# The first block's projections, index scores and choice of keys as one list of tiles, with products by sevens and head roots by logarithms

## The reference

```python
    h = rms_norm(x, norm_w) * (1.0 + scale[:, None, :]) + shift[:, None, :]
    p = h @ w_in
    ...
    q, k, v, gb, iq, ik, iw = jnp.split(pb, DSA_SPLITS, axis=-1)
    q = rms_norm(heads(q), q_gain)
    k = rms_norm(heads(k), k_gain)
    yb = dsa_sparse_attention(q, k, v, iq, ik, iw).reshape(B, S, D_ATT)
    yb = (yb * jax.nn.silu(gb)) @ w_b_out
    gm_a, gm_b = jnp.split(pg, 2, axis=-1)
    merged = jax.nn.sigmoid(gm_a) * ya + jax.nn.sigmoid(gm_b) * yb
```

## Time and profile before

| | us |
|---|---|
| median of three runs | 3241.15 |
| the profiled execution | 3241.27 |
| its span, first to last instruction | 3239.4 |
| TensorE busy in the span | 3051.8 (94%) |
| VectorE busy | 1595.6 (49%) |
| ScalarE busy | 721.5 (22%) |
| mean granted clock of TensorE | 0.988 of full |

### The profile page before, as it was taken

The page is one execution under the profiler, slowest core; times in us unless marked ns, Lnnn a source line. Parts: engine busy times, 40 slices in busy tenths (PEclk is TensorE's granted clock), DMA queues, the critical chain, the costliest instruction groups (busy, mean ns, idle before and its releaser), DMA issues.

```text
span 3239.4 us, 41104 instructions
## 1 busy us (share of the span) xinstructions
PE 3051.8 (94%) x17188; PEld 1833.3 (57%) x17188; DVE 1595.6 (49%) x2499; ACT 721.5 (22%) x1220; POOL 9.6 (0%) x10
## 2 busy tenths in 40 slices
PE   7999999999998899998998998999999999999998
PEld 3476544577446633322332323587577887887875
DVE  4553249655957612222221121546586767576664
ACT  3110232413037110100000000100441333241413
POOL 0000000000000000000000000100000000000000
PEclk9999999999999899999999999999999999999999
DMA  8301144131203499999999999322112212221210
GB/s 282 130 3 54 53 162 176 58 117 64 78 23 118 172 428 428 427 428 428 428 428 428 427 428 416 141 78 98 57 53 78 78 53 78 74 83 53 79 52 27
DMA packets 122072, 588.20 MB, mean 182 GB/s; under 512 B 6944, under 2 KB 9248, under 8 KB 97696
## 3 DMA queue, kind: packets, MB, share of 16 engines
q1 hardware_dynamic: 121888, 585.57, 45.3%
HBM read 583.45 MB, written 2.10 MB: 181 GB/s over the span
## 4 chain that ended last, share of the span: by engine, by line
PE 74%; DMA 16%; DVE 7%; ACT 2%; issue 1%; SPq 0%; DVEq 0%; ACTq 0%
PE ps L579 25%; PE ps L594 20%; DMA work<-in_w_up 7%; PE ps L2724 6%; DMA weight_ring<-in_w_up 5%; PE ps L2805 4%; DMA spare_slot<-in_w_up 3%; PE ps L598 2%; PE ps L2687 2%; PE ps L1389 2%; PE ps L3414 1%; PE ps L1914 1%; PE ps L1903 1%; PE ps L3434 1%; PE ps L3399 1%
## 5 line engine op out<-in xcount | busy, mean ns | idle before, releaser
L594 PE MATMUL ps<-hT,weight_ring 128*128 128x512 f32 (+1 forms) x1016 | 448.9, 598 | 2.9 <-ACT work L707 1.2
L594 PEld LDWEIGHTS ps<-hT,weight_ring 128*128 128x128 f32 (+1 forms) x1016 | 191.5, 191 | 238.2 <-issue 233.3
L365 DVE TENSOR_TENSOR work<-work,ps 128x512 f32<-128x512 f32 x203 | 139.4, 687 | 228.6 <-PE ps L579 224.3
L579 PE MATMUL ps<-weight_ring 128*128 128x256 f32 x992 | 224.8, 379 | 0.0
L2724 PE MATMUL ps<-work 128*64 128x512 f32 x832 | 189.3, 597 | 23.9 <-DMA work<-in_w_up 16.6
L594 PE MATMUL ps<-work,weight_ring 128*128 128x512 f32 (+1 forms) x496 | 211.1, 572 | 0.0
L2889 DVE SCALAR_TENSOR_TENSOR xT<-ps,mod,xT 128x512 f32<-128x512 f32 x128 | 96.1, 751 | 232.3 <-PE ps L2738 222.5
L2724 PE MATMUL ps<-weight_ring,work 128*64 128x512 f32 x800 | 183.4, 602 | 22.4 <-DMA weight_ring<-in_w_up 13.3
L579 PEld LDWEIGHTS ps<-weight_ring 128*128 128x128 f32 x992 | 186.9, 190 | 24.8
L579 PE MATMUL ps<-weight_ring,spare_slot 128*128 128x256 f32 x800 | 181.6, 380 | 0.0
L579 PE MATMUL ps<-hT,weight_ring 128*128 128x256 f32 x736 | 167.2, 383 | 6.3 <-DVE hT L800 3.8
(11 more groups left out here) (491 smaller groups left out, 4266.8 us busy)
## 6 DMA issues: line engine op xcount, KB each, us to landing
work<-in_w_up SPq DMA_DIRECT2D x27, 2048.0 KB, 42.9
weight_ring<-in_w_gate SPq DMA_DIRECT2D x26, 2048.0 KB, 45.2
work<-in_w_gate SPq DMA_DIRECT2D x25, 2048.0 KB, 45.2
weight_ring<-in_w_down SPq DMA_DIRECT2D x24, 2048.0 KB, 43.8
weight_ring<-in_w_up SPq DMA_DIRECT2D x24, 2048.0 KB, 42.4
work<-in_w_down SPq DMA_DIRECT2D x24, 2048.0 KB, 45.0
weight_ring<-in_w_in_odd SPq DMA_DIRECT2D x20, 2048.0 KB, 7.8
weight_ring<-in_w_in SPq DMA_DIRECT2D x16, 2048.0 KB, 11.1
```

The costliest lines, as they stand in the source:

```text
L365: v(dve.tensor_tensor(out, x, got, op), sig if out is steps[-1][0] else None)
L579: ins = pe.matmul(bank[:, j * L:(j + 1) * L], st, mv, start=k == 0, stop=k == 3)
L594: ins = pe.matmul(bank[0:m, 0:f], w[:, k, where:where + m], src[:, k, 0:ntok], start=k == 0, stop=k == kt - 1)
```

## The change

```diff
-        summed = [own - 4, own - 3, own, own + 1, out, out + 1] + [last + i for i in EVEN_SUMMED] + [last + 15 + i for i in ODD_SUMMED]
+        summed = [own - 20, own - 16, own - 13, own - 10] + [own - 4, own - 3, own, own + 1, out, out + 1] + [last + i for i in EVEN_SUMMED] + [last + 15 + i for i in ODD_SUMMED]
...
+def head_norm_logs(ch, beside, places, tiles, mask, width, bank, sq, rt, eps_col=0):
...
+    def total(i):
+        def part(pe):
+            pe.wait_ge(squares.sem, squares.at(i + 1))
+            if i >= 2:
+                pe.wait_ge(roots.sem, roots.at(i - 1 + (4 if i > 5 else 0)))
+            pe.matmul(ps[:, bank + i % 2, :], ch.m(mask), sq[:, i % 4, :], start=True, stop=True).then_inc(sums.sem, 1)
+            sums.total += 1
+        return part
+
+    def log(i):
+        def part(a, act):
+            a.after(sums, i + 1)
+            if i >= 4:
+                a.after(normed, i - 3)
+            a(act.activation(rt[:, i % 4, :], ps[:, bank + i % 2, :], ACT.Ln, bias=ch.eps[:, eps_col:eps_col + 1],
+                             scale=1.0 / width), roots)
+        return part
+
+    def root(i):
+        def part(a, act):
+            a(act.activation(rt[:, i % 4, :], rt[:, i % 4, :], ACT.Exp, scale=-0.5), roots)
+        return part
+
+    def scale(i):
+        def part(v, dve):
+            x, gain = tiles[i]
+            v.after(roots, 4 * (i // 4) + 5 + i)
+            v(dve.scalar_tensor_tensor(x, x, gain, rt[:, i % 4, :], MUL, MUL), normed)
+        return part
+    for i, n in enumerate(places):
+        beside.add(n, total(i), log(i))
+        if i + 1 < len(tiles):
+            beside.add(n, None, square(i + 1))
+        if i % 4 == 3:
+            for k in range(i - 3, i + 1):
+                beside.add(n, None, root(k), scale(k))
...
-    tiles = [(0, "T", j * P, ch.hT, T, act_to(gate[:, j, :], ACT.Silu)) for j in range(4)]
-    tiles += [(1, "T", j * P, ch.hT, T, copy_to(iq[:, j, :])) for j in range(4)]
-    keyed = (keys_and_weights, None)
-    tiles += [(2, "T", 0, ch.hT, T, keyed)]
-    tiles, n = modulated(ch, tiles, 3, bands2(ch, 5, 10))
+        a(act.copy(iw, ch.ps[:, 5, 0:32]))
+    bands = bands2(ch, 5, 9) + bands2(ch, 9, 10) + gate_bands(ch) + bands2(ch, 10, 12)
+
+    def plain(b, j, part):
+        return (b, "T", j * P, ch.hT, T, part)
+
+    queries = [plain(0, j, copy_to(iq[:, j, :])) for j in range(4)]
+    keyed = plain(2, 0, (keys_and_weights, None))
+    gates = [plain(4, j, act_to(gate[:, j, :], ACT.Silu)) for j in range(4)]
+    tiles, staged_at, merges = [], [], []
     beside = Beside()
-    weights_at = next(i for i, t in enumerate(tiles) if t[5] == keyed)
-    head_norm(ch, beside, list(range(8)),
-              [(ch.slot(i)[:, j, :], ch.v(g)) for i, g in ((9, "q_gain"), (10, "k_gain")) for j in range(4)],
-              "blk64", HD, 6, ch.slot(0), ch.slot(1))
-    beside.add(weights_at + 2, turn_weights, take_weights)
-    beside.project(ch, n, tiles, banks=6)
+
+    def rows(b):
+        staged_at.append(len(tiles))
+        tiles.append((b, "M", 0, None, T, copy_to(ch.mstage[:, (len(staged_at) - 1) % 4, :])))
+
+    def turn(i):
+        tiles.append(turn_beside_choice(ch, bands[i], i % 4, staged_at[i]))
+
+    def opened(b, dst, before, function):
+        n = seven(b, dst)
+        for step, quarter in quarters_done(1):
+            beside.add(n + step, scalar=silu_quarter(ch, dst[quarter], before + step, function))
+
+    def seven(b, dst, **how):
+        n, made = len(tiles), tiles[:]
+        seven_tiles(ch, made, b, False, dst, **how)
+        tiles.extend(t[0:3] + (ch.hT,) + t[4:] for t in made[n:])
+        merges.append(n)
+        return n
+    seven(0, quarters(iq), plain_first=True)
+    rows(1)
+    tiles.append(keyed)
+    turn(0)
+    rows(3)
+    opened(4, quarters(gate), 6, ACT.Silu)
+    turn(1)
+    rows(5)
+    rows(6)
+    turn(2)
+    turn(3)
+    opened(7, quarters(ga[:, 0:4, :]), 12, ACT.Sigmoid)
+    rows(8)
+    rows(9)
+    turn(4)
+    turn(5)
+    opened(10, quarters(ga[:, 4:8, :]), 18, ACT.Sigmoid)
+    rows(11)
+    rows(12)
+    rows(13)
+    turn(6)
+    turn(7)
+    turn(8)
+    head_norm_logs(ch, beside, list(range(8)),
+                   [(ch.slot(i)[:, j, :], ch.v(g)) for i, g in ((9, "q_gain"), (10, "k_gain")) for j in range(4)],
+                   "blk64", HD, 6, ch.slot(11), ch.slot(8))
+    beside.add(tiles.index(keyed) + 1, turn_weights, take_weights)
+    dot, relu, add = dsa_scores(ch)
+    query_at, gate_at, first_at, second_at = merges
+    for i in range(24):
+        beside.add(gate_at + (i // 2 - 1) / 2, dot(i), relu(i), add(i))
+    steps = dsa_select(ch)
+    places = [gate_at + 6] * 20 + [first_at + 1 + i // 2 for i in range(12)] + [second_at - 1] * 3
+    places += [second_at + 1 + i // 2 for i in range(12)]
+    for where, step in zip(places + [len(tiles) - 1] * len(steps), steps):
+        beside.add(where, vector=step)
+
+    ch.keep_parts(ch.spare[:, :], [ch.W[:, 0, :], ch.W[:, 1, :]])
+    ch.counter("h_sums")
+    used = ch.used
+    beside.vector[-1] = seq(weight_sum(ch, used, 0), weight_sum(ch, used, 1), activation_sum(ch, 0), activation_sum(ch, 1),
+                            weight_sum(ch, used, 2), activation_sum(ch, 2), weight_sum(ch, used, 3), activation_sum(ch, 3))
+    for n in range(4):
+        beside.add(gate_at - 1, vector=weight_sum(ch, used + 4, n))
+        beside.add(gate_at + 1 + n, vector=weight_sum(ch, used + 7, n))
+        beside.add(first_at + 1 + n, vector=weight_sum(ch, used + 10, n))
+    beside.project(ch, 14, tiles, banks=3)
+    return ga
...
+    def dot(i):
+        def part(pe):
+            s, h = units[i]
+            if i >= 2:
+                pe.wait_ge(relus.sem, relus.at(i - 1))
             rows, n = slice(64 * (h % 2), 64 * (h % 2) + 64), P * (s + 1)
...
-            + weave(blocks(w, 3712, 4736) + joined(w, [(4736, 4808)]), m[5:10])
-            + weave(blocks(w, 4808, 5832), ada[4:6]) + m[10:12] + blocks(A["w_a_out"], 0, 1024)
+            + blocks(w, 4224, 4736) + [m[5]] + joined(w, [(4736, 4808)]) + [m[6]] + blocks(w, 3712, 4224) + m[7:9]
+            + blocks(w, 4808, 5320) + [m[9], ada[4]] + blocks(w, 5320, 5832) + [ada[5]] + m[10:12]
+            + blocks(A["w_a_out"], 0, 1024)
```

More of the change, by code:

```diff
@@ L2078, in scalar, with add, part @@
                 a.after(added, i - 3)
-            n = P * (s + 1)
-            a(act.activation(rel[:, i % 4, 0:n], ps[:, 4 + i % 4, 0:n], ACT.Relu, scale=HD ** -0.5), relus)
-    def row(s):
-        def part(v, dve):
-            for h in range(8):
-                i = 8 * (s - 1) + h
-                v.after(relus, i + 1)
-                n = P * (s + 1)
-                w = iw[:, 8 * s + h:8 * s + h + 1]
-                if h == 0:
-                    v(dve.tensor_scalar(score[:, s, 0:n], rel[:, i % 4, 0:n], w, None, MUL), added)
-                else:
-                    v(dve.scalar_tensor_tensor(score[:, s, 0:n], rel[:, i % 4, 0:n], w, score[:, s, 0:n], MUL, ADD),
-                      added)
+            n = P * (units[i][0] + 1)
+            a(act.activation(rel[:, i % 4, 0:n], ps[:, 3 + i % 2, 0:n], ACT.Relu, scale=HD ** -0.5), relus)
+        return part
+    def add(i):
+        def part(v, dve):
+            s, h = units[i]
+            v.after(relus, i + 1)
+            n = P * (s + 1)
+            w = iw[:, 8 * s + h:8 * s + h + 1]
+            if h == 0:
+                v(dve.tensor_scalar(score[:, s, 0:n], rel[:, i % 4, 0:n], w, None, MUL), added)
+            else:
+                v(dve.scalar_tensor_tensor(score[:, s, 0:n], rel[:, i % 4, 0:n], w, score[:, s, 0:n], MUL, ADD), added)
         return part
-    return tensor, scalar, seq(*[row(s) for s in range(1, 4)])
+    return dot, relu, add
 def dsa_select(ch):
@@ L2103, in dsa_select, with begin, part, best_eight @@
     best = ch.sm[:, 152:160]
[L2105 to L2115 removed]
+    def begin(s):
+        def part(v, dve):
+            if s == 1:
+                v(dve.tensor_copy(bias[:, 0, 0:P], ch.m("adm")))
+            last = score[:, s, P * s:P * (s + 1)]
+            v(dve.tensor_tensor(last, last, ch.m("adm"), ADD))
+        return part
+    def best_eight(s):
+        def part(v, dve):
+            row = score[:, s, 0:P * (s + 1)]
+            v(dve.max(best, row))
+            v(dve.match_replace(row, best, row, -3e38))
+        return part
+    def bias_of(s):
+        def part(v, dve):
+            v(dve.tensor_scalar(bias[:, s, 0:P * (s + 1)], score[:, s, 0:P * (s + 1)], -2e38, -BIG, ALU.is_gt, MUL))
+        return part
+    return [step for s in range(1, 4) for step in
+            [seq(begin(s), best_eight(s))] + [best_eight(s)] * (P // 8 - 2) + [seq(best_eight(s), bias_of(s))]]
 def dsa_attention(ch, tiles):
```

49 lines of the change are left out of this document (17 added, 32 removed).

## The result

Ten timed runs of the kernel after took 3245.40 to 3251.25 us, median 3248.07, and ten of the kernel before 3235.39 to 3243.51, median 3240.32: a ratio of 1.0023, 95% interval 1.0015 to 1.0031. The forecast was 3239.1 with a range to 3247. The profiled execution of after has a span of 3247.7, against 3239.4.

A forecast was written before the change was run, and what follows sets the result against it. TensorE was taken to bound the first stage and VectorE the choice of keys. The attention would start at 165.7 instead of 167.9 us into the stretch, so 3241.3 - 2.2 = 3239.1 us, range 3231 to 3247.

The forecast's parts named there:

- score pairs: Gate block: 24 half-row score products run two at once between tiles, 9.3 us in all, ends 7.7 and 15.5.
- TensorE's products and the first part: First part of the stretch: seven products at 3.47 us each make 24.3 a block; the part ends at 43.9.
- The wait for a square: First part, head norm: the first four Exp hold up a square, so TensorE waits 0.5 us.
- Waits (1) to (3) of the gate block: Gate block, TensorE: 1.8 us for a late weight sum, 2.9 behind a SiLU and table load, 1.7 at half clock.
- Choice and end: Choice of keys starts at 85.3, VectorE ends at 164.0, ScalarE's last turned rows at 165.6, attention starts at 165.7.
- its wait for product 6: Second merge block: ScalarE's row copies queue behind a sigmoid, so VectorE waits 1.1 us for this product.
- the second rival: Merge blocks: TensorE's clock falls to 1.2 GHz and stays down, VectorE waits 7.9 us instead of 1.1; 3247.6, chance 0.14.
- I let the 2.2 us pass through: Stages after the attention's start: they wait for the work before them, so the 2.2 us gain reaches the end.
- the gate block at its floor: Gate block without its waits, pairs for 7.7: TensorE ends it at 75.9, choice 8.4 us sooner; 3230.7, chance 0.20.
- The clock's rival: Merge blocks: half clock through products 1 and 6 of the second adds 6.8 us, gate block 1.7; 3247.6, chance 0.14.

The follow-up runs named there:

- fours: Kernel after with its 24 score products placed four at a time in four banks, instead of two at a time in twelve places; ratio to before 1.0004.
- gate_order: Kernel after with the gate block's four weight sums ahead of the first two score additions, and early SiLU quarters behind the last relu; ratio to before 0.9996.
- before_padded: Kernel before with useless instructions added (57 VectorE, 152 TensorE records), moving later code to where it lies in the kernel after; ratio to before 1.0013.
- before_vector_padded: Kernel before with only the 57 useless one-column clears on VectorE added, no products on TensorE; ratio to before 1.0002.
- logs_only: Kernel before with only the head roots changed, to Ln and Exp on ScalarE without reciprocals; ratio to before 1.0008.

## Why the prediction was wrong

It failed at two steps. The score pairs were priced too low, and with them the stretch lost 2.0 us where 2.2 were to be gained. And stages with equal work were taken to need equal time, without a reason given; they took 6.5 us more.

- **TensorE's products and the first part**: right. 3.455 us from one product to the next (3.47 in the forecast), and the first part ended at 43.8, forecast 43.9. The wait for a square was 0.3, forecast 0.5. The Trainium skill, "ScalarE: Activation LUTs", section "Table sets: the hidden batching unit", gives ln and then exp one load; the trace of after speaks against that, as the earlier trace rows did:

```profile
415.30 0.69 ACT L1734 ACTIVATE work<-ps,eps 128x512 f32<-128x512 f32 x1 [2.96 <-PE ps L1725]
...
416.66 1.28 ACT L1740 ACT_TABLE_LOAD   x1
417.96 2.62 ACT L1740 ACTIVATE work<-work 128x512 f32<-128x512 f32 x4
420.59 1.28 ACT L1734 ACT_TABLE_LOAD   x1
421.89 0.69 ACT L1734 ACTIVATE work<-ps,eps 128x512 f32<-128x512 f32 x1
```

  L1734 is the Ln, L1740 the Exp, and each change between them has its load of 1.28.
- **Score pairs**: the term that was mis-sized. 9.3 us were taken between 7.7 and 15.5; 12.5 were measured, 3.2 more. The 0.1 for a switch came from a misread row (58.24 in the earlier trace rows). Its 1.92 us are one visit of two pairs, so the 0.2 over its columns were divided by two, and the half tile behind it, which took 3.63 for 3.44, was left out. Counted from visit to visit the switch there and back is 0.4, as fours showed by halving the visits.
- **Waits (1) to (3) of the gate block**: right in place and size, 1.5 for 1.8, 2.5 for 2.9, and 2.2 for 1.7 at half clock, where a pair ran slow as well (1.58 for 1.06). The block took 43.2 us for 40.0, the difference in the pairs.
- **Choice and end**: the choice started at 88.6, forecast 85.3. VectorE's sum held (62.4, 10.2, 5.0), but its wait for product 6 was 2.55, forecast 1.1: the product before it ran at half clock (5.08 for 3.6), behind a wait of TensorE of 2.52. That is the second rival's mechanism in small. Together 3.3 + 1.4 made VectorE end late, at 168.6 for 164.0. What the attention waited for were ScalarE's last copies, 169.9 for 165.6, 4.3 late. VectorE was busy 92% of the choice, where over 95% was forecast.
- **"I let the 2.2 us pass through"**: half right. What changes the start of the attention does pass through (gate_order, fours). What failed is the silent other half, that equal work in later stages takes equal time. The change's added instructions moved all later code; before_padded, without the change, lost 5.3 us in the rest that way. The 1.1 left of the 6.5 are no more than two executions of one kernel differ by.
- **The rivals**: the gate block at its floor was not what came, but its account of the waits was sound: without them gate_order ended the block at 80.6, near the rival's 75.9 and the 4.8 that the pairs cost more (12.5 for 7.7). The clock's rival gave 3247.6, near the result by luck: it lost 1.4 us at product 6 where the rival had 6.8, and most of the measured loss lies behind the stretch, where no rival had any.

## What to carry to other kernels

A change that adds or removes instructions moves the code of every later stage. Here that alone was worth 2.6 us (before_vector_padded) to 5.3 us (before_padded) in stages nobody touched, more than the change did to its own stretch: measure the changed stretch from its own start and the rest apart, and add idle instructions to before, before you judge an edit of a few us. On an engine that waits in order, put what others wait for (sums, relus) ahead of what only comes early (SiLU quarters), and send small products of another shape in few, long visits. Where VectorE carries the stage, whole tiles can beat seven products, since the products' sums and additions are VectorE's and the waits that they give TensorE were followed by half clock here. And take the price of a switch from one visit to the next, with the work between, not from the visit's own row.

## What the hardware showed

- One load of instructions of 16384 bytes for 256 TensorE records; where one lay 3 to 5 us behind the issue of two transfers (2 MB and 384 KB), they landed in 9.2 and 9.7 us instead of 7.9 and 8.4. Of the transfers behind 566 us that normally land in 7 to 9 us, all 44 with such a load 2 to 6 us behind their issue were over 0.8 us late in the 14 traces, and none of 408 without a load.
- A VectorE instruction right behind a wait, with a record number that leaves 63 when divided by 128, began 0.28 to 0.38 us later than with another number, in 31 of 32 cases. The copy near 2540 is one, late in five kernels.
- A wait of 1.58 us before 2573 left TensorE's clock at 2.4 GHz, one of 1.94 or 1.95 at the same place was followed by 3.4 us at 1.2 GHz, in seven kernels (1.58 to 1.60) and in five. So 0.35 us of delay on VectorE cost 2.0 us. No length of wait holds for all places: near 3195 one of 1.38 left the clock up in before and one of 1.39 was followed by 3.4 us at 1.2 GHz in logs_only.
- Going from products of all rows to a pair of half-row products and back cost 0.4 us, whatever the width.
- Work ahead of the stretch that no edit touched ended anywhere between 394.3 and 399.7 us.
